# A fused transformer block on one core: attention passes begun inside the projections before them, and the modulation sums kept as rows

## The reference, cut to what matters

```python
mod   = silu(c) @ ada_w + ada_b                     # 6 * 2048 columns: sh1, sc1, g1, sh2, sc2, g2
h, hc = modulate(rms_norm(x), sh1, sc1), modulate(rms_norm(ctx), csh1, csc1)
qa, ka, va, qb, kb, vb, gates = split(h @ w_in)     # each 1024 wide, gates 4096; hc gives k and v too
a = neighbourhood_attention(qa, ka, va, ctx keys and values, rpb)       # 8 heads of 128
b = differential_attention(rope(qb), rope(kb), vb, ctx, lam)            # 8 heads, two maps of 64
#   p = softmax(s0) - lam * softmax(s1); o = p @ v; then an RMSNorm of each head's output
y = sigmoid(gates_a) * (a @ w_pa) + sigmoid(gates_b) * (b @ w_pb)
x = x + g1 * (y @ w_out)
x = x + g2 * conv_ffn(modulate(rms_norm(x), sh2, sc2))
return rms_norm(x)
```

## Time and profile before

| | us |
|---|---|
| median of 3 runs (lowest, highest) | 1760.55 (1760.33, 1763.31) |
| the profiled execution: time | 1760.43 |
| its span (first to last instruction) | 1758.8 |
| PE busy | 1700.5 (97%) |
| DVE busy | 1092.5 (62%) |
| ACT busy | 754.6 (43%) |
| POOL busy | 105.5 (6%) |

### The profile page before, as it was taken

The page is one execution under the profiler, slowest core; times in us unless marked ns, Lnnn a source line. Parts: engine busy times, 40 slices in busy tenths (PEclk is TensorE's granted clock), DMA queues, the critical chain, the costliest instruction groups (busy, mean ns, idle before and its releaser), DMA issues.

```text
span 1758.8 us, 23861 instructions
## 1 busy us (share of the span) xinstructions
PE 1700.5 (97%) x8831; PEld 1395.9 (79%) x8831; DVE 1092.5 (62%) x1380; ACT 754.6 (43%) x956; POOL 105.5 (6%) x155
## 2 busy tenths in 40 slices
PE   4999999999999899999999999999999999999997
PEld 1468888878888668888888788888888888888885
DVE  1348768867774884554555566666666666655556
ACT  2232224622223465444444455555555555444444
POOL 0003221222210000000000000000000000000000
PEclk9999999999999999999999999999999999999999
DMA  9999888279874307666665556666666666655551
GB/s 354 387 383 336 277 284 291 79 250 342 277 244 132 97 21 237 191 187 193 189 212 193 160 170 190 188 187 189 185 188 188 186 188 191 201 191 192 193 194 66
DMA packets 160716, 369.31 MB, mean 210 GB/s; under 512 B 11471, under 2 KB 12127, under 8 KB 159758
## 3 DMA queue, kind: packets, MB, share of 16 engines
q1 hardware_dynamic: 139808, 291.98, 51.3%
q0 software_dynamic: 19728, 72.04, 12.3%
q10 hardware_dynamic: 1118, 4.44, 0.6%
HBM read 366.26 MB, written 2.16 MB: 209 GB/s over the span
## 4 chain that ended last, share of the span: by engine, by line
PE 87%; DMA 5%; DVE 5%; issue 1%; ACT 1%; SPq 0%; ACTq 0%; DVEq 0%; POOL 0%; POOLq 0%
PE ps L1677 20%; PE ps L1676 10%; PE ps L1686 10%; PE ps L1688 10%; PE ps L1687 10%; PE ps L1996 4%; PE ps L1998 4%; PE ps L1997 4%; DMA raw<-in_ada_w 3%; PE ps L1601 3%; PE ps L1602 2%; PE ps L1603 2%; DMA ada_raw<-in_ada_w 2%; PE ps L1673 1%; PE ps L1593 1%
## 5 line engine op out<-in xcount | busy, mean ns | idle before, releaser
L993 DVE TENSOR_TENSOR w_lo<-raw,w_hi 128x1024 fp32r<-128x1024 f32 x480 | 584.8, 1224 | 455.8 <-ACT w_hi L595 454.8
L595 ACT CAST w_hi<-raw 128x1024 fp32r<-128x1024 f32 x480 | 503.4, 1049 | 844.8 <-PE ps L1688 329.1
L1677 PE MATMUL ps<-h2T,w_hi 128*128 128x512 f32 x1320 | 463.2, 394 | 0.0
L1676 PE MATMUL ps<-h2T,w_lo 128*128 128x256 f32 x1320 | 367.0, 278 | 0.0
L1677 PEld LDWEIGHTS ps<-h2T,w_hi 128*128 128x128 f32 x1320 | 248.0, 188 | 53.6
L1676 PEld LDWEIGHTS ps<-h2T,w_lo 128*128 128x128 f32 x1320 | 248.5, 188 | 4.2
L1686 PE MATMUL ps<-w_hi,hT 128*128 128x512 f32 x512 | 200.7, 392 | 0.0
L1688 PE MATMUL ps<-w_hi,hT 128*128 128x512 f32 x512 | 199.4, 389 | 0.0
L1687 PE MATMUL ps<-w_lo,hT 128*128 128x512 f32 x512 | 199.2, 389 | 0.0
L1065 DVE SCALAR_TENSOR_TENSOR ada_acc<-ada_raw,silu_c,ada_acc 128x512 f32<-128x512 f32 x240 | 180.1, 751 | 28.2 <-DMA ada_raw<-in_ada_w 10.3
L1996 PE MATMUL ps<-w_hi,f_hi 128*128 128x512 f32 x352 | 137.0, 389 | 1.0 <-DVE conv_in L1422 1.0
(11 more groups left out here) (217 smaller groups left out, 1960.9 us busy)
## 6 DMA issues: line engine op xcount, KB each, us to landing
raw<-in_ffn_w_up SPq DMA_DIRECT2D x176, 512.0 KB, 3.8
raw<-in_w_in SPq DMA_DIRECT2D x152, 512.0 KB, 4.6
ada_raw<-in_ada_w POOLq DMA_DIRECT2D x128, 512.0 KB, 5.9
raw<-in_ffn_w_down SPq DMA_DIRECT2D x88, 512.0 KB, 4.4
raw<-in_ada_w SPq DMA_DIRECT2D x64, 512.0 KB, 10.6
raw<-in_w_out SPq DMA_DIRECT2D x32, 512.0 KB, 3.7
raw<-in_w_branch_a SPq DMA_DIRECT2D x16, 512.0 KB, 3.6
raw<-in_w_branch_b SPq DMA_DIRECT2D x16, 512.0 KB, 3.7
```

Source lines behind the costliest of these rows:

```text
L595: act.copy(w_hi[:, s % SPLIT_SLOTS, :], raw[:, s, :]).then_inc(hi_ready[s], 1)
L993: dve.tensor_tensor(w_lo[:, s % SPLIT_SLOTS, :], raw[:, s, :], w_hi[:, s % SPLIT_SLOTS, :], ALU.subtract).then_inc(lo_ready[s], 1)
L1676: pe.matmul(ps[:, b + t, 0:SEQ], w_lo[:, row4(s), at], high(kc), start=False, stop=False)
L1677: mm = pe.matmul(o, w_hi[:, row4(s), at], both(kc), start=False, stop=(kc == KC - 1))
```

## The change

1. The order of the projections becomes k, q, v, q, k, v in both halves, so that job 5 and job 11 are the second halves of v, and heads 0 to 3 have their q, k and v before.
2. The first part of each pass runs inside job 5 or 11: scores of n = 0 and 1 after the last tile of slot 5, turn 0 after slot 6, turn 1, values 0, values 1 with scores 2, and scores 3 after the four tiles of slot 7. The last part (values 14, turn 15, values 15) runs between tiles of job 6 or 12. In between stand n = 2 to 14.
3. The result of the last v job is read in four pieces, one bank each. Some banks of the pass change (`na_banks`, `df_banks`).
4. The DVE loop of the differential pass is shortened: the scale 1/8 goes into q, the first map is no longer normalised (the second gets the weight -lam * sum0/sum1, and the output of n is multiplied by 1/sum0 when it is read, by ACT for even and DVE for odd n).
5. The steps of the modulation sums are dealt out by number, not by group (`ADA_STEPS`): 12, 34, 13, 37, 32 in jobs 1 to 5, 24, 13, 28, 13, 32, 18 in jobs 6 to 11.
6. `sum_mod` has 32 columns of ones as weights and the accumulated tile moving: 4 products of 128 columns into the four quarters of the partitions of a bank. ACT copies the row sums and stores them to DRAM by its own queue (11 stores); later POOL loads them as 64 rows of 128, DVE adds the bias, one transpose gives the columns, and the two gate rows go through DRAM and back by a broadcasting DMA. 32 transposes and 5 copies of 128 x 512 or more go.
7. All rotations are in jobs 8, 10 and 11; the split of `aT` moves from job 11 to job 12/13 behind that of `bT`.

```diff
-PROJECTIONS = [("k", KA), ("k", KA + GROUP), ("v", VA), ("v", VA + GROUP), ("q", QA), ("q", QA + GROUP),
+PROJECTIONS = [("k", KA), ("q", QA), ("v", VA), ("q", QA + GROUP), ("k", KA + GROUP), ("v", VA + GROUP),
...
-ADA_JOBS = [1, 1, 2, 2, 3, 3, 4, 5, 6, 6, 7, 7, 8, 8, 9, 9]
+ADA_STEPS = {1: 12, 2: 34, 3: 13, 4: 37, 5: 32, 6: 24, 7: 13, 8: 28, 9: 13, 10: 32, 11: 18}
+ADA_SPAN = {JOB_DIFF - 1: range(6), JOB_DIFF: range(3, SLOTS), JOB_MERGE - 1: range(4)}
...
# PE: sum_mod
-                for n in range(TILES):
-                    mm = pe.matmul(ps[:, b, col + n:col + n + 1], ada_acc[:, g % 2, n * P:(n + 1) * P], ones[:],
-                                   start=True, stop=True)
+                for n, at in enumerate(PIECE_AT):
+                    mm = pe.matmul(ps[at:at + 32, b, col:col + P], sum_ones,
+                                   ada_acc[:, g % 2, n * P:(n + 1) * P], start=True, stop=True)
...
# PE: the neighbourhood pass
+            def first_na(s, t):
+                if (s, t) == (5, 3):
+                    pe.wait_ge(*results_read(JOB_DIFF - 2))
+                    na_scores(0)
+                    na_scores(1)
+                if (s, t) == (6, 3):
+                    na_turn(0)
+                if (s, t) == (7, 0):
+                    na_turn(1)
+                if (s, t) == (7, 1):
+                    na_values(0)
+                if (s, t) == (7, 2):
+                    na_values(1)
+                    na_scores(2)
+                if (s, t) == (7, 3):
+                    na_scores(3)
+            def last_na(s, t):
+                if (s, t) == (0, 0):
+                    na_values(N - 2)
+                    na_turn(N - 1)
+                if (s, t) == (0, 2):
+                    na_values(N - 1)
+            projection(JOB_DIFF - 1, first_na)
+            for n in range(EARLY, N - 1):      # EARLY = 2; scores(n+2), values(n-1), turn(n) as before
...
+            projection(JOB_DIFF, last_na)
# PE: the differential pass has the same form (first_df); its scores 0 wait for sums_read of all 16 groups
# PE: gates
-                        for kc in range(KC):
-                            mm = pe.transpose(ps[:, 4 + kc // 4, (kc % 4) * P:(kc % 4 + 1) * P],
-                                              mod[:, kc:kc + 1].to_broadcast([P, P]), ident)
-                        mm.then_inc(g1_spread, 1)
+                        pe.wait_ge(mod_full, 1)
+                        pe.transpose(ps[:, 4, 0:MOD_ROWS], mod_part[:], consts[0:MOD_ROWS, 0:MOD_ROWS])\
+                            .then_inc(mod_turned, 1)
...
-            pe.wait_ge(x2_added, 2 * TOK)
-            for q in range(4):
-                for kc in range(4 * q, 4 * q + 4):
-                    mm = pe.transpose(ps[:, q, (kc % 4) * P:(kc % 4 + 1) * P],
-                                      mod[:, 3 * KC + kc:3 * KC + kc + 1].to_broadcast([P, P]), ident)
-                mm.then_inc(g2_spread, 1)
...
# ACT: differential pass
+            df_exponents(0)
+            round_hi(JOB_MERGE, 0)
+            df_exponents(1)
+            df_read_turned(0)
+            round_hi(JOB_MERGE, 1)
+            df_read_turned(1)
+            df_result(0)
+            round_hi(JOB_MERGE, 2)
+            df_exponents(2)
+            for t in (0, 2, 3):
+                read_values(last, t, kv_read)
+            for n in range(EARLY, N):
+                if n + 1 < N:
+                    df_exponents(n + 1)
+                if n == EARLY:
+                    read_values(last, 1, kv_read)
+                df_read_turned(n)
+                if n % 2:
+                    df_result(n - 1)
...
# DVE: differential pass, one n
-                dve.reciprocal(row_sum[:, n % 3, :], row_sum[:, n % 3, :]).then_inc(df_recip, 1)
-                dve.tensor_scalar(row_sum[:, n % 3, 1:2], row_sum[:, n % 3, 1:2], lam[:, 0:1], None, ALU.mult)
-                dve.tensor_scalar(diff_e[:, n % 2, 0, :], diff_e[:, n % 2, 0, :], row_sum[:, n % 3, 0:1], None,
-                                  ALU.mult).then_inc(df_first, 1)
+                dve.reciprocal(row_inv[:, n % 3, :], row_sum[:, n % 3, :]).then_inc(df_recip, 1)
+                dve.tensor_scalar(weight, row_inv[:, n % 3, 1:2], lam[:, 0:1], row_sum[:, n % 3, 0:1], ALU.mult,
+                                  ALU.mult).then_inc(df_lam, 1)
                 dve.scalar_tensor_tensor(diff_e[:, n % 2, 0, :], diff_e[:, n % 2, 1, :], weight,
                                          diff_e[:, n % 2, 0, :], ALU.mult, ALU.add).then_inc(df_probs, 1)
-                dve.tensor_scalar(row_max[:, n % 3, :], row_max[:, n % 3, :], DIFF_SCALE, None, ALU.mult)
```

More of the change, by code:

```diff
@@ L118, in turn_bank, with ada_schedule, sum_schedule, sums_of @@
     return 7 - kc % 2
-ADA_JOBS = [1, 1, 2, 2, 3, 3, 4, 5, 6, 6, 7, 7, 8, 8, 9, 9]
-ADA_GROUPS = len(ADA_JOBS)
-ADA_BEFORE_NA = sum(j < JOB_DIFF for j in ADA_JOBS)
+ADA_STEPS = {1: 12, 2: 34, 3: 13, 4: 37, 5: 32, 6: 24, 7: 13, 8: 28, 9: 13, 10: 32, 11: 18}
+ADA_SPAN = {JOB_DIFF - 1: range(6), JOB_DIFF: range(3, SLOTS), JOB_MERGE - 1: range(4)}
+ADA_GROUPS = 4 * D // GROUP
+ADA_BEFORE_NA = sum(n for j, n in ADA_STEPS.items() if j < JOB_DIFF) // KC
+SUM_AFTER = (1, 3, 5)
+def ada_schedule():
+    slots, step = {}, 0
+    for j, n in ADA_STEPS.items():
+        span = ADA_SPAN.get(j, range(SLOTS))
+        for i, s in enumerate(span):
+            last = step + (i + 1) * n // len(span)
+            first = step + i * n // len(span)
+            slots[j, s] = [divmod(at, KC) for at in range(first, last)]
+        step += n
+    return slots
+ADA_SLOT = ada_schedule()
+def sum_schedule():
+    done = {g: at for at, steps in ADA_SLOT.items() for g, kc in steps if kc == KC - 1}
+    sums = {}
+    for g in range(ADA_GROUPS):
+        j, s = done[g]
+        later = [n for n in SUM_AFTER if n > s and (j != JOB_DIFF - 1 or n < 5)]
+        at = (j, later[0]) if later else (j + 1, SUM_AFTER[0])
+        if j == JOB_MERGE - 1:
+            at = (j, 4)
+        sums.setdefault(at, []).append(g)
+    return sums
+ADA_SUMS = sum_schedule()
+SUM_STORES = len({j for j, _ in ADA_SUMS})
+def sums_of(j):
+    return [g for (job, _), groups in ADA_SUMS.items() if job == j for g in groups]
 ADA_FIRST_COL = 2 * D
+MOD_ROWS = 4 * KC
+MOD_COL = SEQ
+EARLY = 2
 C_IDENT, C_ROT, C_COS, C_SIN, C_MASK = 0, 128, 256, 512, 768
@@ L247, in block_program @@
     row_sum = keep("row_sum", [P, 3, 2])
+    row_inv = keep("row_inv", [P, 3, 2])
     lam = keep("lam", [P, 2])
@@ L421, in results_read, with tiles_read @@
             n = sum((kind == "q") == mine for kind, _ in PROJECTIONS[:j - JOB_NA + 1])
+            if not mine and j >= JOB_DIFF:
+                n += 2 * TOK - 1
             return (q_read if mine else kv_read), n
-        def ada_groups(j):
-            return [g for g, job in enumerate(ADA_JOBS) if job == j]
+        def tiles_read(j, tiles):
+            return kv_read, results_read(j)[1] + tiles - 1
         def ada_bank(j):
@@ L1272, in _ @@
+                    if j == last and s in (4, 5):
+                        rope(s + 2)
+            df_difference(0)
+            split_lo(JOB_MERGE, 0)
+            df_difference(1)
+            split_lo(JOB_MERGE, 1)
+            split_lo(JOB_MERGE, 2)
+            df_maxima(2)
+            df_result(1)
+            df_difference(2)
+            df_maxima(3)
+            df_maxima(4)
+            for n in range(EARLY + 1, N):
+                df_difference(n)
                 if n + 2 < N:
                     df_maxima(n + 2)
-                if n in LATE_ROTATIONS:
-                    rope(LATE_ROTATIONS[n])
```

523 lines of the change are left out of this document (317 added, 206 removed).

## The result

| | before | after |
|---|---|---|
| median of 4 runs each, same chip (lowest, highest) | 1760.76 | 1738.7 (1736.93, 1739.74) |
| the profiled execution | 1760.43 | 1738.52 |
| its span | 1758.8 | 1736.8 |

The ratio is 0.9867, 95% interval 0.9851 to 0.9882. The forecast was 1744.7 with a range of 1737 to 1753: direction and range hold, but the gain is 22.0 (by the spans) where 15.7 was forecast.

What follows compares the result with a forecast made beforehand. The prediction took PE, busy for 97% of the span, as the bound, with DVE bounding the differential pass. Gains of -19.3 and costs of +3.6 made -15.7, 1744.7 us; own range 1739 to 1749, wider range 1737 to 1753.

Steps and rivals of the forecast that it cites:

- Sums, -3.4: Modulation sums on PE: the 32-column form costs 0.70 instead of 0.91 us each, 16 sums, gain 3.4 (bounds 2.1 to 6.5).
- Neighbourhood pass, -4.1: Parts moved into jobs 5 and 6 cover PE's waits: 7.7 us of stalls and slow clock become 3.6, gain 4.1.
- Differential pass, -9.0: Shorter DVE loop makes PE the bound, period 2.90 to 2.6; waiting falls from 14.1 to 5.1 us, gain 9.0.
- Returns, +1.0: Ten more returns of PE to ordinary weights after other products, 0.1 us lost each: +1.0 (0 to 2).
- The clock, +1.5: One fall of the clock kept, after the new stall at the differential start: +1.5 us (0 to 3).
- Gates -1.6 and +0.3: One transpose replaces g1's 16 in job 13, 1.6 us gained; removing g2's 16 before the second norm costs 0.3.
- mod wait -1.2: PE's wait of 1.2 us for `mod` goes, as ACT reads the sums ahead of PE's need.
- late slot +0.8: Dealt-out modulation steps fill DVE evenly in the jobs and just hold; 0.8 us left for a late slot (0 to 6).
- (a): Rival: differential period stays near 2.85 and both starts are twice as long, 1751 us; chance 0.24 together with (d).
- (c): Rival: DVE can't carry the dealt-out modulation steps, +24 or so, 1768 us; chance 0.07.
- (d): Rival: early steps wait for the job's end; only DVE loop, gates and sums gain, 1750 us; 0.24 together with (a).
- (b): Rival: everything short goes well, sums at 0.5, no fall of the clock, starts hidden, 1736 us; chance 0.09.

Runs made afterwards that it cites:

- experiment 1: Changed kernel with the modulation sums' products back in their old form (accumulated tile as weights, one column of ones moving): 1744.63 us.
- experiment 10: Kernel before, with only the short DVE loop of the differential pass added: 1756.73 us, ratio 0.9971.
- experiment 9: Kernel before, with only the new order of the neighbourhood projections (v last) and modulation groups dealt anew by whole groups: 1768.06 us, ratio 1.0036.
- experiment 8: Changed kernel with eight modulation steps moved from job 5 to job 4 (45 and 24 in place of 37 and 32): 1741.15 us.
- experiment 2: Changed kernel with the neighbourhood pass whole again behind job 5, except scores 0 and 1, which stay after slot 5: 1740.17 us.
- experiment 4: Changed kernel with one more DVE instruction (first map multiplied by 1.0) in each n of the differential loop: 1741.47 us.

## Why the prediction was right, and where it was wrong

What bounds: right. PE's own time and PE's waits were the right account, and every large gain is in them.

**Sums, -3.4: too small, 5.8 by rows and by experiment 1.** This term was mis-sized. I stayed near the head's row (0.78 for 256 columns) and took 0.70; the rows after have 0.55. The switch costs what the earlier trace rows said, 0.19 in both directions. The inside fell from 0.56 to 0.36 with half the columns, near the far bound named. The Trainium skill, "TensorEngine Tiling (Array Packing)", section Tiling Modes, says that a change of mode drains the engine. On the way in the trace agrees: the last ordinary matmul takes 0.32 in front of sums, of 64-row scores and of the one 64-row transpose, and 0.23 in front of transposes, values and rotations that fill the array. The way back does not tell: behind values and transposes, which change no mode, the second matmul comes 0.08 late, nearly the 0.10 of a sum. That page does not decide how the inside scales.

**Neighbourhood pass, -4.1: the size near, the reason wrong, and in part luck.** The products of this pass take 5.2 less. Of the new stalls I had 3.0 at the start and 0.7 in the tail (written as 3.6 in sum). The start has 0.4 + 1.0 = 1.4, the tail 0.7; the 0.9 for the load of the bias, which I had not seen, brings them to 3.0. And the step "it only covers waits" failed: the cut is worth 1.5, the tail 1.8 less 0.35 for the start. The half clock behind the old stall was 1.6 in the trace of before; experiment 10 shows that the same stall may come without it, so no part of the change can be credited with all of it. The order is worth 1.2 at equal clock (experiment 9). I had written that the order of the projections moves no work of PE and left it there. It moves the work of the others: with q last, the third split for job 6 ended only 1.9 us before the end of job 5, bias and maxima began behind it, and ACT's and DVE's reading of q (1.0 and 1.2) stood ahead of the first probabilities.

**Differential pass, -9.0 with +1.5 for the clock: 8.8, the half clock in it, rotations counted.** The loop was the best step: period 2.59 (taken 2.6), PE end to end. I priced it at 0.3 in 11 n, 3.3; experiment 10 has 5.6: eight steady periods give 2.6, the period behind the late rotation 1.2, start and end of the pass, which I had not counted, 1.9. The start stall I had at 3.0; it is 2.0, in the engine named. The cut is worth 1.3, the tail's 1.8 less 0.55 for the start. The remaining 1.9 of the 8.8 belong to the order and to the rotations that left the pass; they were not taken apart.

**Returns, +1.0.** Ordinary matmuls took 1.5 us more in sum. In this are the sums' ways in (16 x 0.09 = 1.5) and, with the other sign, the 1.2 of the `mod` wait, so some 1.2 is left for the new returns. The sum is near, but not its terms: between job 1 and job 14 there are 15 more returns than before, not ten. Behind neighbourhood scores and rotations the second matmul comes 0.42 after the first, behind differential scores 0.34, behind values and transposes 0.31, where I had 0.35 for all. Before, behind the same neighbourhood scores and rotations in q jobs, it came 0.30 to 0.31 after the first; no run tells what makes the difference. By these distances over the usual 0.23 the new returns cost about 2; what offsets the rest was not taken apart. In part the moved products are cheaper inside a job, which I had not seen: values 0 stand 0.81 before the next matmul (311.99 to 312.80), in the rhythm 0.97 (324.72 to 325.69).

**The clock, +1.5.** One fall where I put it, worth 1.6. That it came was likely and not certain: the stall of 2.03 stands in six traces, and the half clock follows in five of them, not in that of experiment 8.

**Gates -1.6 and +0.3, mod wait -1.2, late slot +0.8.** The first and third are right (1.5; no such wait). The second norm takes 7.8 us before and after: the 16 transposes taken from it cost and gained nothing. No slot was late in the changed kernel; experiment 8 shows that 8 steps more in job 4 are too many.

The surplus of 6.3: sums 2.4, neighbourhood pass 1.1, differential pass with its clock 1.3, late slot 0.8, second norm 0.3, less 0.2 for the returns and 0.1 for the gates; and 0.6 between second norm and down projection, a distance that varies by 1.4 (491.7 to 493.1) among the traces of kernels that don't differ there, so the change is not shown to have any part in it. That is 6.2 of the 6.3. Most terms erred to the same side, and the range held them with 1.7 to spare. Rivals: (a) is excluded by the period, (c) by the absence of waits for `w_lo`, (d) by the early turns and values, which stand inside jobs 5 and 11; (b), 1736 with a chance of 0.09, named the sums rightly and the starts wrongly.

## What to carry to other kernels

A job that runs ahead of a latency-bound pass is chosen by what it leaves on the other engines' queues, not by its work on PE: last should come the one whose result is read late and by the engine that has time. Undo each part alone before crediting it, and compare traces at equal clock and equal waits for loads. Two parts here were told as one idea; as a cut it was worth 1.5 and 1.3 us a pass, all of it the tail, and as an order 1.2 in one pass, while the order with whole groups of old sums made the old kernel slower. The stall of 2 us was worth breaking up: as 0.5 and 0.8 it had no half clock behind it in two traces, though as 1.1 and 0.8 it had in two of three.

## What the runs showed of the hardware

- The same stall of 2.03 us at the differential start was followed by 3.4 us at a granted clock of 0.50 (1.2 GHz) in five traces (the changed kernel twice, experiments 1, 2 and 4) and by none in experiment 8; in the changed kernel one period then took 4.20 instead of 2.58. The stall of 2.42 at the old neighbourhood start was followed by it in the kernel before and not in experiment 10. Waits of 0.5 and 0.8 were followed by none in two traces; waits of 1.1 and 0.8 by half clock in two of three.
- The way from ordinary matmuls into products of another tiling (128x32, 64x128, 64x64) costs 0.32 from start to start, into others of 128x128 0.23.
- Eight records of a 32-column product took 0.36 with 128 moving columns and 0.56 with 256, plus 0.09 in and 0.10 back.
- Scaling 128x512 in place on DVE is recorded at 0.43 by a constant and 0.47 by a column of factors, but it took DVE 0.35 where the next instruction didn't need the result and 0.58 where it did.
- The differential rhythm was 2.58 to 2.59 in the eleven traces with the short DVE loop; with one DVE instruction more in each n the last periods were 2.77 on average.
- A load of 96 KB for the position bias kept DVE waiting 0.8 to 2.1 us at one place in the middle of the neighbourhood pass of all fourteen traces, and one period of PE was 0.1 to 1.7 us longer for it.
